# A gated scan rewritten as two skewed pair streams, with compact states and half-width levels

## The reference

```python
def step(state, inp):
    qc, kc, vc, lf = inp
    a = jnp.cumsum(lf, axis=2)
    a_last = a[:, :, -1:, :]
    s_new = jnp.exp(a_last)[:, :, 0, :, None] * state + jnp.einsum(
        "bhsk,bhsv->bhkv", kc * jnp.exp(a_last - a), vc)
    inter = jnp.einsum("bhtk,bhkv->bhtv", qc * jnp.exp(a), state)
    diff = a[:, :, :, None, :] - a[:, :, None, :, :]
    dec = jnp.exp(jnp.where(causal, diff, -jnp.inf))
    scores = jnp.einsum("bhtk,bhsk,bhtsk->bhts", qc, kc, dec)
    intra = jnp.einsum("bhts,bhsv->bhtv", scores, vc)
    return s_new, inter + intra
```

## Time and profile before

| | us |
|---|---|
| median of three runs | 6555.46 |
| lowest and highest | 6535.63, 6560.89 |
| span of the profiled execution | 6529.7 |
| TensorE busy in it | 5885.4 (90%) |
| VectorE busy | 2844.0 (44%) |
| ScalarE busy | 1763.7 (27%) |
| GpSimd busy | 328.0 (5%) |

### The profile page before, as it was taken

The page is one execution under the profiler, slowest core; times in us unless marked ns, Lnnn a source line. Parts: engine busy times, 40 slices in busy tenths (PEclk is TensorE's granted clock), DMA queues, the critical chain, the costliest instruction groups (busy, mean ns, idle before and its releaser), DMA issues. The chain is left out here.

```text
span 6529.7 us, 77413 instructions
## 1 busy us (share of the span) xinstructions
PE 5885.4 (90%) x30276; PEld 4344.2 (67%) x30276; DVE 2844.0 (44%) x6558; ACT 1763.7 (27%) x4082; POOL 328.0 (5%) x381
## 2 busy tenths in 40 slices
PE   5879998989969999799999988969998899999889
PEld 2338887765548666567777466867666667775667
DVE  2220124433334666625555035345667535551254
ACT  2221015431134000114444123042000134442231
POOL 0000110000010000210000000000000300000000
PEclk8989998857779978799999999989898999999999
DMA  4001110134320000000000111220000000001212
GB/s 158 13 13 50 35 60 28 55 131 136 130 87 20 1 7 1 11 14 1 1 1 1 47 49 49 97 87 14 1 7 1 20 4 1 1 1 33 63 49 94
DMA packets 145404, 256.78 MB, mean 39 GB/s; under 512 B 10796, under 2 KB 89748, under 8 KB 144276
## 3 DMA queue, kind: packets, MB, share of 16 engines
q1 hardware_dynamic: 107700, 211.98, 9.3%
q10 hardware_dynamic: 37344, 39.85, 1.8%
HBM read 195.81 MB, written 55.98 MB: 39 GB/s over the span
## 5 line engine op out<-in xcount | busy, mean ns | idle before, releaser
L1903 PEld LDWEIGHTS ps_pv<-y_t,probs_t 128*128 128x128 f32 x4640 | 588.6, 192 | 153.3 <-issue 142.9
L1980 DVE TENSOR_REDUCE soft<-ps_scores 128x1 f32<-128x512 f32 (+1 forms) x648 | 410.3, 633 | 495.8 <-PE ps_scores L1866 494.7
L1903 PE MATMUL ps_pv<-y_t,probs_t 128*128 128x64 f32 x4640 | 579.7, 270 | 31.4 <-DVE y_t L2018 30.8
L1419 PEld LDWEIGHTS ps_s<-qf,kb 64*128 64x128 f32 x4032 | 423.1, 214 | 194.5 <-DVE products L1532 127.0
L1419 PE MATMUL ps_s<-qf,kb 64*128 64x128 f32 x4032 | 472.8, 315 | 8.6 <-DVE scores_t L1541 8.5
L1277 DVE TENSOR_TENSOR features_low<-h_t,features_high 128x1024 fp32r<-128x1024 f32 x260 | 304.0, 1171 | 354.6 <-ACT features_high L1242 354.1
L644 PE MATMUL ps_proj<-weight_ring,h_t 128*128 128x256 f32 x2048 | 448.5, 381 | 2.7 <-PE ps_proj L644 2.2
L644 PEld LDWEIGHTS ps_proj<-weight_ring,h_t 128*128 128x128 f32 x2048 | 388.9, 191 | 57.6 <-issue 5.4
L1959 ACT ACTIVATE probs<-ps_scores,soft 128x512 f32<-128x512 f32 (+1 forms) x648 | 407.6, 642 | 16.6 <-DVE soft L1989 16.6
L1214 PE MATMUL ps_proj<-features_high,weights_high 128*128 128x512 f32 (+1 forms) x880 | 346.2, 393 | 60.1 <-DVE features_low L1277 30.8
L1945 ACT ACTIVATE probs_t<-ps_pt 128x512 f32<-128x512 f32 (+1 forms) x392 | 205.0, 523 | 686.3 <-PE ps_pt L1883 676.2
(11 more groups left out here) (308 smaller groups left out, 9159.0 us busy)
## 6 DMA issues: line engine op xcount, KB each, us to landing
weight_ring<-in_w_in_dram SPq DMA_DIRECT2D x40, 1024.0 KB, 6.4
mod_weights<-in_w_mod_dram ACTq DMA_DIRECT2D x24, 1024.0 KB, 5.2
x_rows<-h_rows SPq DMA_DIRECT2D x32, 512.0 KB, 5.9
t_rows<-t_rows SPq DMA_DIRECT2D x64, 256.0 KB, 2.6
x_res<-h_rows SPq DMA_DIRECT2D x32, 512.0 KB, 3.5
res<-result SPq DMA_DIRECT2D x48, 264.0 KB, 2.0
res_rows<-res SPq DMA_DIRECT2D x48, 264.0 KB, 3.9
h_t<-v_rows SPq DMA_DIRECT2D x3, 4096.0 KB, 13.8
```

What stands on the lines that cost most here:

```text
L1419: mm = pe.matmul(pS[pr][h][:, cs], kb[lo:lo + HD, pr, cs], rhs, start=True, stop=True)
L1903: mm = pe.matmul(pv[:, 0:HD], pT[:, before(u, c) % 4, j * P:(j + 1) * P], VN[:, k0 + k, kv * HD:(kv + 1) * HD], start=(k == 0), stop=(k == ...
L1980: dve.tensor_reduce(st[:, u % 2, 0, c:c + 1], ps[c][:, 0:tiles(u, c) * P], AXX, ALU.max).then_inc(mx.h, 1)
```

## The change

`stage_hgrn_scan` is written anew. Its arithmetic is the same.

- *Two skewed streams.* Each pair runs through eleven phases a step: eight levels (0 to 7), turn (8), state (9), outputs (10). Every engine follows the same list of slots, in which pair 1 is five phases behind pair 0. All semaphores are doubled, one for each pair. The projection of the next step stands behind phases 1 to 4, two k at a time. It and the turned keys and the state's new part share the bank `ps_f`; `f` and `kb` have two buffers each, so the two copies into working tiles are gone.
- *Heads alternate*, block by block, in the scores. *Half-width levels:* only the half of the query columns that a level keeps is computed (64 moving columns for 128), and copied.
- *Last levels by ScalarE:* of phases 6 and 7, whole rectangles are copied by ScalarE, six small copies a pair, without a mask. `scores_t` is cleared once at a call's start, and TensorE and ScalarE wait for that (`state_zero`).
- *Products on GpSimd:* seven multiplications a pair and step, started when the states of the step before are up.
- *Compact states:* 64 columns for both heads, one update per block in place of two, in a ring of eight, so that the outputs no longer alternate with the updates. All outputs of a step and pair are one group.
- The mask table shrinks from 16 x 128 to 2 x 6 x 64 columns. In the second block's layers each stage gives its semaphores back (`env.stage()`).

```diff
+        def slots():
+            for at in range(NSTEP * PH + SKEW):
+                for pr in range(2):
+                    x = at - SKEW * pr
+                    if 0 <= x < NSTEP * PH:
+                        yield (pr, *divmod(x, PH))
...
+            def level(s, pr, ph):
...
+                else:
+                    pe.wait_ge(up[pr].h, up[pr].at(8 * s + ph))
+                    if ph <= 6:
+                        pe.wait_ge(cp[pr].h, cp[pr].at(6 * s + ph))
+                    else:
+                        pe.wait_ge(ca[pr].h, ca[pr].at(2 * s + 1))
+                for i in range(n):
+                    for h in range(2):
+                        lo = slice(HD * h, HD * (h + 1))
+                        q = qT[lo, pr, col + i * P:col + (i + 1) * P] if ph < 2 else qf[lo, pr, i * P:(i + 1) * P]
+                        mm = pe.matmul(pS[pr][h][:, i * HB:(i + 1) * HB].rearrange("p (b x) -> p b x", x=x),
+                                       kb[lo, s % 2, pr, i * P:(i + 1) * P],
+                                       q.rearrange("p (b a x) -> p b a x", a=2, x=x)[:, :, half, :], start=True, stop=True)
+                mm.then_inc(sc[pr].h, 1)
...
+            for pr, s, ph in slots():
+                if ph < 8:
+                    level(s, pr, ph)
+                elif ph == 8:
+                    turn(s, pr)
+                elif ph == 9:
+                    state(s, pr)
+                else:
+                    outputs(s, pr)
+                if s + 1 < NSTEP and 1 <= ph <= 4:
+                    project(s + 1, pr, (2 * ph - 2, 2 * ph - 1))
...
+            def products(s, pr):
+                pool.wait_ge(ready[pr].h, ready[pr].at(2 * s + 2))
+                if s >= 1:
+
+                    pool.wait_ge(su[pr].h, su[pr].at(blocks_to[s]))
+                for l in range(7):
+                    if l >= 1:
+                        pool.wait_ge(pd[pr].h, pd[pr].at(7 * s + l))
+                    p2 = prod(s, pr, l).rearrange("p (b a) -> p b a", a=2)
+                    pool.tensor_tensor(prod(s, pr, l + 1), p2[:, :, 0], p2[:, :, 1], ALU.mult).then_inc(pd[pr].h, 1)
...
+            dve.memset(sT[:, :, :, :], 0.0)
+            dve.memset(st[:, :, 0, :], 0.0).then_inc(env.sem("state_zero").h, 1)
...
+                elif ph < 8:
+                    raise_q(s, pr, ph - 1)
+                    raise_k(s, pr, ph - 1).then_inc(up[pr].h, 1)
+                    if ph <= 5:
+                        keep(s, pr, ph)
+                elif ph == 9:
+                    dve.wait_ge(um[pr].h, um[pr].at(s + 1))
+                    dve.wait_ge(pd[pr].h, pd[pr].at(7 * s + 7))
...
+                elif ph == 10 and d == 1:
+                    dve.wait_ge(om[pr].h, om[pr].at(s + 1))
```

More of the change, by code:

```diff
@@ L66, in retire, with stage @@
         self.free += [self.sems.pop(n) for n in names]
+    @contextmanager
+    def stage(self):
+        before = set(self.sems)
+        yield
+        self.retire(*sorted(n for n in self.sems if n not in before and n not in LASTING))
     def sb(self, ctx, name, shape, dt=F32):
@@ L1457, in _ @@
+            for pr in range(2):
+                pe.wait_ge(om[pr].h, om[pr].at(NSTEP))
             pe.sem_inc(env.sem("w_used").h, 1)
@@ L1485, in stage_hgrn_scan @@
[L1485 to L1494 removed]
+                act.wait_ge(pj[pr].h, pj[pr].at(s + 1))
@@ new lines, in keep @@
+            def keep(s, pr, ph):
+                n = steps[s][1]
+                x = 1 << max(ph - 1, 0)
+                half = kh if ph == 0 else qh
+                shape = [P, n, HB // x, x]
+                for h in range(2):
+                    dst = sT[:, pr, h, 0:n * P].rearrange("p (i b a x) -> p i b a x", i=n, a=2, x=x)[:, :, :, half, :]
+                    src = pS[pr][h][:, 0:n * HB].rearrange("p (i b x) -> p i b x", i=n, x=x)
+                    mask = env.levmask[:, d, ph, :].rearrange("p (b x) -> p b x", x=x)[:, None, :, :].to_broadcast(shape)
+                    ins = dve.copy_predicated(dst, mask, src)
+                ins.then_inc(cp[pr].h, 1)
```

385 lines of the change are left out of this document (196 added, 189 removed).

## The result

The changed kernel takes 6375.2 us (median of four runs, 6355.2 to 6379.9) where the kernel before took 6545.6 beside it (four runs, 6517.3 to 6560.9): a ratio of 0.973, with a 95% interval of 0.970 to 0.976. The forecast was 6360. Its profiled execution spans 6378.1 us where the one before spans 6529.7; a run's own time is 1.8 us over its span in both.

What follows compares the result with a forecast made beforehand. TensorE, busy for 90% of the span, was taken as the bound. Four scan calls falling from 1107.3 to 920 us, plus 2 for the mask, saved 189 of 6529.7: 6341; 25.8 from span to median gave 6366, stated as 6360, range 6240 to 6490.

Steps and rivals of the forecast that it cites:

- the half width: Score groups with 64 moving columns: no gain taken, since weight loads set the pace; bounds nothing and 112 us in all.
- an allowance for the clock: Scan calls: a mean granted clock near 0.88 turns 204 us into 204 / 0.885 = 230 per call.
- Alternating heads: 16-record score groups: two streams of eight side by side, 1.16 us to the end; TensorE held 1.04 in place of 1.64.
- The slots at full clock: TensorE's time summed over paired phases plus waits: a four-block step takes 40.5 us against 54.
- a call at full clock: One scan call: start, steps and last phases sum to 198 us, with 6 more 204.
- the 6 us set aside for loose ends: Added per call for VectorE's sum into y_t, the bounds of layer 1 and semaphore gaps.
- rival 1: Scan calls: the clock stays at half, a call takes 346 us, total 6830, slower; chance 0.08.
- 1.4 us a phase: VectorE per phase of a pair: two raises and two half-width copies, in place of 2.3 us with products.
- ScalarE, GpSimd: Last levels' small copies and the products (2.4 us per pair and step) hide under other work: nothing added.
- rival 3: GpSimd and VectorE shut each other out in the scan: 135 of 189 us saved are gone, 6495; chance 0.06.
- Tail and skew: Step's end: about 6 us in which little else ran now has five phases of the other pair beside it.
- Start and mask: Call's start: memsets add 2 us before the first projection's 7.14, 9.3 in all; smaller mask saves 2 us once.

Runs made afterwards that it cites:

- e7: The changed kernel with scores at full width (128 moving columns) again, copies still taking the half they need: 6244.5 us, 0.955 of the kernel before.
- f8_dense: e7 with copies of the first three levels from and to contiguous runs, leaving scores in wrong places: 6229.2 us, 0.952 of the kernel before.
- e6_spread: The changed kernel with the next step's projection spread over phases 0 to 5 instead of 1 to 4: 6268.1 us, 0.958 of the kernel before.
- g1_full_no_alt: e7 with all blocks of head 0 before head 1 (heads not alternating): 6378.6 us, 0.977 of the kernel before.
- g2_half_late: The changed kernel with full-width scores in phases 0 to 4, half-width only in 5 to 7: 6249.9 us, 0.957 of the kernel before.

## Why the prediction was right, and where it was not

The time lay 15 us over the forecast, the direction was right, and the main reason given for it held. One term was wrong in kind, the half width, and an allowance for the clock, made without it, happened to take in most of what it cost.

**Alternating heads: right.** 1.11 to 1.16 us for a group, as worked out, and 132 us in the calls. What the forecast did not see is that this edit alone would bring the old order of work to 917.6 us, and to 0.95 of the clock.

**The slots at full clock: right to a percent.** e7, which runs at 0.98, is what the forecast called "a call at full clock": 204.7 us against 204. A four-block step took 40.66 against 40.5. Up to the first cut of a full step it is 70.5 us where the slots give 69.4; from the cut in the last full step to the end 53.3 where they give 48, which the 6 us set aside for loose ends take in. Some luck is in it: VectorE's slow first copies, which the sum had not, cost 6 us a call (f8_dense, where they are fast, has 198.8), and that is about all that the 6 had to take in.

**Half width: the step that failed.** "Half width saves nothing" is nearly true of a group (0.05 us). But I bounded the term by nothing and a gain of 112, and wrote that a loss would need a slow strided read of the columns. The loss came by the granted clock, and it is 119 us, more than the best gain that I had allowed for and on the other side. Half width stood only in rival 1 as a danger to the clock, with a chance of 0.08; it belonged in the sum, as a term of its own beside the slots without projections. How far it is the number of columns, and how far their gaps, stays open.

**The clock: mis-sized; right on the place, without the condition.** I took 0.885 and had 0.78 to 0.83. I blamed the slots and the last step without projections. That is where it falls, and it no longer does where e6_spread fills the slots. But it takes the half width as well: in e7 the same slots and the same last step run at 1.00. The attention that was granted 1.00 with 64-column matmuls, my argument against rival 1, does not carry over to half-width scores. On the other hand 0.79 would, by my division, have meant 258 us a call; it was 235. The three calls at 0.78 and 0.79 are 15 to 17% longer than e7's, not 25%. Two rows say where a part of the difference is: a group of scores takes 1.95 us at half clock against 1.11, 1.8 times and not twice, and in the second call TensorE is idle for 20.3 us (238.2 less 217.9), in e7's for 24.8 (204.9 less 180.1). So a clock off by 0.1 cost just 18 us in the sum (938 against 920), and that is luck: two errors that offset each other in part.

**VectorE: right in phases 3 to 5, short in phases 0 to 2.** 1.4 us a phase became 1.94 where runs are of one or two elements. It cost 24 us in the calls.

**ScalarE, GpSimd: right.** Both hide; in e7's first call TensorE waits 1.3 us for ScalarE's blocks. The full exclusion of rival 3 would have put 90 us of VectorE's time behind GpSimd's products in the four calls. Measured are 3.4 us for the raises of the first call, which would be 14 in four. Meetings are few, and my sum took all of GpSimd's time for one. A single raise beside a product took 0.83 us in place of 0.42. Its end lies 0.28 us behind the product's end, and in the earlier trace rows the raise of 0.58 ends 0.27 us behind the GpSimd operation's, which I had read as less than a full wait. The next raise there ran undelayed (0.41) inside a GpSimd operation that took 1.97 us where one of its shape had taken 0.77, so the wait can fall on GpSimd as well. The rule on the shared port pair ("SBUF — State Buffer", "Who interferes with whom" in the Trainium skill) is of single instructions that overlap in time, one of which has the pair to itself until it ends; these rows agree with it, and are too few to prove it.

**Tail and skew: the cover was overpriced.** The forecast gained much from five phases of the other pair at a step's end. The skew as such is worth 0.8 us a full step and loses 15 us in all. Which of the other edits at a step's end shortened it was not tried by itself.

**Start and mask: nearly right.** The memsets take 1.76 and 0.17 us, and TensorE begins 2.05 us after the first of them begins; its first projection then takes 8.8 us rather than 7.1, so the start is 10.9 us where I took 9.3. The masks' cast ends 2.3 us earlier than before, where I took 2.

**Span to median.** I added 25.8 us, the distance of the median from one profiled span. A run is 1.8 us over its own span; the rest was chance between runs. Without it the forecast would have been 6343, and the 17.7 us lost in the attention, which no edit here touches, came on the other side.

The parts, in us of the four calls: alternation 1107.3 to 917.6; the rest of the rewrite, at full width, 917.6 to 818.8; half width 818.8 back up to 938.0. The shares hang on the order in which one takes them: with the rest of the rewrite first, it is 1107.3 to 951.3 (g1_full_no_alt), and the alternation is 951.3 to 818.8.

## What to carry to other kernels

Before a rewrite, run its smallest part alone: three lines gave more than the rewrite as it stood. When an edit halves the columns of a matmul whose weight load stays the same, look at the granted clock of the stretch, not only at the length of a group; the group was 0.05 us shorter and the program 117 us longer. If the narrow matmuls must stay, keep wider ones between them. Where float32 matmuls use different rows of the array, let them alternate in the queue.

## What the runs showed of the hardware that I had not expected

- Half-width score groups lower the granted clock from 0.98 to between 0.78 and 0.83 where they follow one another; with a block of the projection in each slot the clock was 1.00 for 153.6 us on end (first call of e6_spread), and mixed with full-width groups 0.96 to 0.97 over a call (g2_half_late).
- Alternating heads raised the granted clock, in the kernel before from 0.84 to 0.92 up to 0.95 to 0.97, in the new one at full width from 0.94 to 0.98.
- The last step of a call ran at 1.00 in e7 with TensorE busy for 26.2 of 34.1 us, and at 0.79 in the kernel before with 42.6 of 49.
- A masked copy of 128x256 float32 takes 0.42 us into runs of four elements and more, and 0.74 into runs of one or two with gaps; gaps in its PSUM source added nothing.
- Time outside the scan varied by 28 us between executions of these kernels (5412 to 5440 us), most of it in the dilated attention.
